# One joint gather of U and V rows, worked row by row, in the expert layer of a hybrid decoder trunk

## The reference

```
idx  = take_along_axis(cand_i, pos)            # token, head, 16 experts
gate = softmax(top_s)
act  = gelu(einsum('td,thkd->thk', xt, expert_u[idx]))
out  = einsum('thk,thkd->td', gate * act, expert_v[idx])
```

## Time and profile before

| | us |
|---|---|
| median of 3 runs | 4101.56 (4099.58 to 4101.72) |
| the profiled execution | 4101.73 |
| its span, first to last instruction | 4099.8 |

### The profile page before, as it was taken

One profiled execution on the slowest core, in us unless ns is written; L12 is line 12 of the kernel. 1 busy time (PEld: TensorE's weight loads), 2 busy tenths in 40 slices (PEclk: granted clock), 3 DMA queues, 4 the chain that ended last, 5 costly groups with the idle time before them and its releaser, 6 DMA issues. The chain is left out here.

```text
span 4099.8 us, 43527 instructions
## 1 busy us (share of the span) xinstructions
PE 3766.2 (92%) x15978; PEld 2821.7 (69%) x15978; DVE 2532.3 (62%) x5462; ACT 739.8 (18%) x1381; POOL 1789.6 (44%) x1508
## 2 busy tenths in 40 slices
PE   8999999987899999995799999999878999999947
PEld 7856788876666666652688567888766666666526
DVE  4455215838767676877844452158387677668777
...
GB/s 106 113 31 42 58 144 144 134 117 327 409 410 403 409 400 410 406 409 400 235 84 113 31 42 59 145 142 134 124 331 409 410 408 408 402 410 399 409 403 243
DMA packets 332164, 1047.19 MB, mean 255 GB/s; under 512 B 79024, under 2 KB 96048, under 8 KB 313008
## 3 DMA queue, kind: packets, MB, share of 16 engines
...
...
## 5 line engine op out<-in xcount | busy, mean ns | idle before, releaser
L1733 PE MATMUL bank<-v_tile,shared 128*128 128x512 f32 x2048 | 906.2, 597 | 31.9 <-DVE shared L2136 30.2
L2198 POOL DMA_INDIRECT u_rows<-in_peer_u,idx_all x512 | 673.6, 1316 | 541.1 <-DVE act_u L2093 444.5
L2105 DVE SCALAR_TENSOR_TENSOR x<-v_rows,act_w,x 128x1024 f32<-128x1024 f32 x512 | 657.8, 1285 | 349.9 <-DMA v_rows<-in_peer_v,idx_all 331.9
L2093 DVE CUSTOM_DVE_ANT_0 u_rows<-u_rows,h 128x1024 f32<-128x1024 f32 x512 | 610.0, 1221 | 194.8 <-DMA u_rows<-in_peer_u,idx_all 193.1
L1733 PEld LDWEIGHTS bank<-v_tile,shared 128*128 128x128 f32 x2048 | 391.6, 192 | 485.2 <-issue 444.6
L2198 POOL DMA_INDIRECT v_rows<-in_peer_v,idx_all x512 | 560.6, 1095 | 370.7 <-DVE x L2105 275.0
L2208 POOL DMA_INDIRECT first_cells<-first_gate,cell_all x256 | 412.6, 1612 | 593.4 <-DVEq L2085 467.0
L1721 PE MATMUL bank<-hT,bT 128*128 128x256 f32 x2048 | 452.5, 379 | 0.0
L1721 PEld LDWEIGHTS bank<-hT,bT 128*128 128x128 f32 x2048 | 388.4, 190 | 72.0 <-issue 22.0
L1625 PE MATMUL bank<-hT,ring 128*128 128x256 f32 x1536 | 341.6, 383 | 14.3 <-PEq L152 14.2
L1625 PEld LDWEIGHTS bank<-hT,ring 128*128 128x128 f32 x1536 | 293.9, 192 | 56.9 <-issue 16.2
(11 more groups left out here) (406 smaller groups left out, 4547.8 us busy)
## 6 DMA issues: line engine op xcount, KB each, us to landing
v_tile<-in_peer_v SPq DMA_DIRECT2D x256, 512.0 KB, 7.4
...
bT<-in_peer_ut SPq DMA_DIRECT2D x128, 512.0 KB, 8.1
...
```

Of the source, the lines that this page charges most:

```text
L1733: ins = mm(acc[t][part][:, :], act_pair[p % AHEAD][:, at:at + P], v_tile[:, e % DENSE, part * 512:part * 512 + 512], start=(e == 0), stop= ...
L2093: nc.vector.tensor_tensor_reduce(out=u[:, n % RINGS, :], in0=u[:, n % RINGS, :], in1=h[:, t, :], scale=1.0, scalar=0.0, op0=ALU.mult, op1= ...
L2105: stt(out=m.x[:, 2 + t, :], in0=vr[:, n % RINGS, :], scalar=act_w[:, p % 4, i:i + 1], in1=m.x[:, 2 + t, :], op0=ALU.mult, op1=ALU.add).the ...
L2198: nc.gpsimd.indirect_dma_start(out=rows[:, n % RINGS, :], out_offset=None, in_=table, in_offset=bass.IndirectOffsetOnAxis(ap=idx_all[:, t, ...
```

## The change

U and V are concatenated on the host to one table `peer_uv` with rows of 8 KB, and `u_rows` and `v_rows` become five joint buffers `uv_rows` of the same total size. One indirect DMA gathers both halves of a row (1 MB for 128 tokens). A buffer is freed by the add alone. DVE works rows one by one: dot n, then add n - 2 (ROWS_BEHIND = 2), where it did four dots and then four adds of two chunks before. ACT does, for each row, a gelu of one column and then the product with the gate as an activation Copy with a scale; DVE's product L2099 is gone. LAG falls to 1, which ends the list one chunk earlier. POOL's order follows: four joint gathers a chunk. The dense part is as before; it keeps its own tables of U and V.

```diff
--- before.py
+++ after.py
@@ -1394,7 +1394,9 @@
 HOT_CHUNKS = 4
 GATES_AFTER = 9
 CHUNKS_BESIDE = (0, 2, 4)
-LAG = 2
+LAG = 1
+ROWS = CHUNKS * STEP
+ROWS_BEHIND = 2
 CELLS = P * KEYS * P
 CELL_OCT = OCT * P
 LATE_CHUNKS = 4
@@ -1499,13 +1501,12 @@
 
     nc, io = m.nc, m.io
     with ExitStack() as ctx:
-        s = semaphores(m, COMMON + " wg_in keys_in gain_in p_in comb_ready rms_ready h_ready topped exp_done selected u_free v_free "
+        s = semaphores(m, COMMON + " wg_in keys_in gain_in p_in comb_ready rms_ready h_ready topped exp_done selected dotted weighed uv_free "
                        "first_chosen gelu_done out_free ple_rms ple_h ple_added slots_turned slots_here left_ready right_ready hot_filled hot_read "
                        "stored0 stored1 pre_in0 pre_in1 pre_in2 pre_in3 v_in0 v_in1 v_in2 v_in3 gate_in0 gate_in1 "
                        "pre_done pre_read gated v_done dense_added w_in side_sums last_sums last_scaled mix_filled mix_read")
         sb = lambda n, shape, dt=F32: ctx.enter_context(nc.sbuf_tensor(f"{n}_{layer}", shape, dt))
-        u = sb("u_rows", [P, RINGS, D])
-        vr = sb("v_rows", [P, RINGS, D])
+        uv = sb("uv_rows", [P, RINGS, 2 * D])
         h = sb("h", [P, 2, D])
         scores = sb("scores", [P, 4, 2, 2, KEYS])
         shared = sb("shared", [P, AHEAD, 2 * HALF_T])
@@ -1571,7 +1572,7 @@
         gate_in = s.gate_in0, s.gate_in1
         stored = s.stored0, s.stored1
         acc = (m.banks[4], m.banks[5]), (m.banks[6], m.banks[7])
-        tables = io.peer_u.rearrange("l e d -> (l e) d"), io.peer_v.rearrange("l e d -> (l e) d")
+        table = io.peer_uv.rearrange("l e d -> (l e) d")
         cols = lambda half: slice(half * HALF_T, (half + 1) * HALF_T)
         pre_bank = lambda p: m.banks[2 + p % 2 if p else 5]
         late_sum = lambda n: m.banks[4 + n // 2][:, cols(n % 2)]
@@ -1603,7 +1604,7 @@
         def arrivals(n):
 
             k = n % RINGS
-            return 16 * (layer * len(range(k, CHUNKS * STEP, RINGS)) + n // RINGS + 1)
+            return 16 * (layer * len(range(k, ROWS, RINGS)) + n // RINGS + 1)
 
         block = ctx.enter_context(nc.Block())
 
@@ -1904,9 +1905,16 @@
                         f(expo[:, t, :], top[:, t, :], ACT.Exp, bias=ntop[:, t:t + 1], accum_out=den[:, t:t + 1]).then_inc(s.exp_done, 1)
 
             def chunk(c):
-                if c < CHUNKS:
-                    act.wait_ge(s.u_free, STEP * (c + 1))
-                    f(act_g[:, c % 4, :], act_u[:, c % 4, :], ACT.Gelu_apprx_tanh).then_inc(s.gelu_done, 1)
+                if c == CHUNKS:
+                    return
+                for i in range(STEP):
+                    n = c * STEP + i
+                    t, col = slot(n)
+                    one = slice(i, i + 1)
+                    act.wait_ge(s.dotted, n + 1)
+                    f(act_g[:, c % 4, one], act_u[:, c % 4, one], ACT.Gelu_apprx_tanh).then_inc(s.gelu_done, 1)
+                    act.wait_ge(s.gelu_done, n + 1)
+                    f(act_w[:, c % 4, one], act_g[:, c % 4, one], ACT.Copy, scale=gate_all[:, t, col:col + 1]).then_inc(s.weighed, 1)
 
             def slots():
                 act.wait_ge(s.slots_turned, 1)
@@ -2084,29 +2092,31 @@
                     step.step(tt((gate_all if half else first_gate)[:, :, some], expo[:, :, :], over(rden.unsqueeze(2), (P, 2, TOPK)), ALU.mult))
                     v.sem_inc(s.selected if half else s.first_chosen, 1)
 
+            def dot(n):
+                t, _ = slot(n)
+                k = n // STEP % 4
+                v.wait_ge(m.uv_landed[n % RINGS], arrivals(n))
+                nc.vector.tensor_tensor_reduce(out=uv[:, n % RINGS, 0:D], in0=uv[:, n % RINGS, 0:D], in1=h[:, t, :], scale=1.0, scalar=0.0,
+                                               op0=ALU.mult, op1=ALU.add, accum_out=act_u[:, k, n % STEP:n % STEP + 1]).then_inc(s.dotted, 1)
+
+            def add_row(n):
+                t, _ = slot(n)
+                k = n // STEP % 4
+                v.wait_ge(s.weighed, n + 1)
+                if n:
+                    v.wait_ge(s.uv_free, n)
+                stt(out=m.x[:, 2 + t, :], in0=uv[:, n % RINGS, D:], scalar=act_w[:, k, n % STEP:n % STEP + 1], in1=m.x[:, 2 + t, :],
+                    op0=ALU.mult, op1=ALU.add).then_inc(s.uv_free, 1)
+                if n % TOPK == TOPK - 1:
+                    v.wait_ge(s.uv_free, n + 1)
+                    v.sem_inc(s.out_free, 1)
+
             def chunk(c):
-                if c < CHUNKS:
-                    for i in range(STEP):
-                        n = c * STEP + i
-                        t, col = slot(n)
-                        v.wait_ge(m.u_landed[n % RINGS], arrivals(n))
-                        nc.vector.tensor_tensor_reduce(out=u[:, n % RINGS, :], in0=u[:, n % RINGS, :], in1=h[:, t, :], scale=1.0, scalar=0.0,
-                                                       op0=ALU.mult, op1=ALU.add, accum_out=act_u[:, c % 4, i:i + 1]).then_inc(s.u_free, 1)
-                if LAG <= c < CHUNKS + LAG:
-                    p = c - LAG
-                    t, col = slot(p * STEP)
-                    v.wait_ge(s.gelu_done, p + 1)
-                    step.step(tt(act_w[:, p % 4, :], act_g[:, p % 4, :], gate_all[:, t, col:col + STEP], ALU.mult))
-                    for i in range(STEP):
-                        n = p * STEP + i
-                        v.wait_ge(m.v_landed[n % RINGS], arrivals(n))
-                        if n:
-                            v.wait_ge(s.v_free, n)
-                        stt(out=m.x[:, 2 + t, :], in0=vr[:, n % RINGS, :], scalar=act_w[:, p % 4, i:i + 1], in1=m.x[:, 2 + t, :],
-                            op0=ALU.mult, op1=ALU.add).then_inc(s.v_free, 1)
-                    if p % JOB_CHUNKS == JOB_CHUNKS - 1:
-                        v.wait_ge(s.v_free, STEP * (p + 1))
-                        v.sem_inc(s.out_free, 1)
+                for n in range(c * STEP, (c + 1) * STEP):
+                    if n < ROWS:
+                        dot(n)
+                    if ROWS_BEHIND <= n < ROWS + ROWS_BEHIND:
+                        add_row(n - ROWS_BEHIND)
 
             def hot(q):
                 if q == QUADS:
@@ -2187,18 +2197,16 @@
         @block.gpsimd
         def _(pool):
 
-            def fetch(n, free, rows, table, sems):
-                if not 0 <= n < CHUNKS * STEP:
-                    return
+            def fetch(n):
                 t, col = slot(n)
                 if n % TOPK == 0 and t == 0:
                     pool.wait_ge(s.selected, col // TOPK + 1)
                 if n >= RINGS:
-                    pool.wait_ge(free, n - RINGS + 1)
+                    pool.wait_ge(s.uv_free, n - RINGS + 1)
                 nc.gpsimd.indirect_dma_start(
-                    out=rows[:, n % RINGS, :], out_offset=None, in_=table,
+                    out=uv[:, n % RINGS, :], out_offset=None, in_=table,
                     in_offset=bass.IndirectOffsetOnAxis(ap=idx_all[:, t, col:col + 1], axis=0),
-                ).then_inc(sems[n % RINGS], 16)
+                ).then_inc(m.uv_landed[n % RINGS], 16)
 
             def scatter(n):
                 if n % TOPK == 0:
@@ -2214,14 +2222,11 @@
             for n in range(late):
                 scatter(n)
             for n in range(RINGS):
-                fetch(n, s.u_free, u, tables[0], m.u_landed)
-            for n in range(RINGS):
-                fetch(n, s.v_free, vr, tables[1], m.v_landed)
-            for c in range(CHUNKS + LAG):
-                for n in range(STEP * c + RINGS, STEP * (c + 1) + RINGS):
-                    fetch(n, s.u_free, u, tables[0], m.u_landed)
-                for n in range(max(STEP * (c - LAG), 0) + RINGS, STEP * (c - LAG + 1) + RINGS):
-                    fetch(n, s.v_free, vr, tables[1], m.v_landed)
+                fetch(n)
+            for c in range(CHUNKS):
+                begin = STEP * (c + 1) - ROWS_BEHIND - STEP + RINGS
+                for n in range(max(begin, RINGS), min(begin + STEP, ROWS)):
+                    fetch(n)
                 if c < LATE_CHUNKS:
                     for n in range(TOPK // LATE_CHUNKS):
                         scatter(late + c * TOPK // LATE_CHUNKS + n)
@@ -2237,9 +2242,9 @@
         m.nc, m.ctx, m.sems = nc, ctx, []
         names = "loaded stored x_landed0 x_landed1 x_landed2 x_landed3".split()
         m.once = once = namedtuple("Semaphores", names)(*[ctx.enter_context(nc.semaphore(n)) for n in names])
-        swdge = [ctx.enter_context(nc.semaphore(f"{n}_landed{k}")) for n in "uv" for k in range(RINGS)]
+        m.uv_landed = [ctx.enter_context(nc.semaphore(f"uv_landed{k}")) for k in range(RINGS)]
         m.scattered = ctx.enter_context(nc.semaphore("cells_scattered"))
-        m.nc, m.io, m.u_landed, m.v_landed = nc, io, swdge[:RINGS], swdge[RINGS:]
+        m.nc, m.io = nc, io
         m.banks = [ctx.enter_context(nc.psum_tensor(f"bank{k}", [P, 512], F32)) for k in range(8)]
```

(2 more changed lines are left out.)

## The result

The changed kernel takes 4205.1 us (median of four runs, 4197.7 to 4213.0) against 4101.6 us for the kernel before on the same chip: 1.0251 times as long, 95% interval 1.0229 to 1.0273, some 103 us. The sign and the range of the prediction hold, the size doesn't: 42 us were forecast.

What follows compares the result with a forecast made beforehand. PE was taken to set the pace up to about pair 59, then DMA, then DVE. Per layer +7 start, +8 cushion, +6 tail, -3.6 larger pieces, +3.6 slot waits: +21, twice +42 on 4101.7, 4144 us (range 4110 to 4190).

Steps and rivals of the forecast that it cites:

- five buffers are just enough in the dense stretch, with 7% to spare: Dense stretch: a chunk of gathered rows needs 16.7 us with five joint buffers, under PE's 17.9, so PE hides it.
- latency rival: Dense stretch: gathers take 10 to 14 us to land and bound the kernel; about 4260 us, at 12 some 4500; chance 0.18.
- Larger pieces, -3.6: Last nine DMA-bound chunks: 8 KB pieces move 4% faster, saving 3.6 us a layer; elsewhere PE hides the gain.
- Start, +7: Before PE's dense work: six more adds (7.7 us) precede the last one-hot products; +7 us a layer, from -5 to +20.
- the coupling: ACT's in-order list: a chunk's small gelu stands behind a dense gelu that waits for PE's value products.
- Cushion, +8: Last dense pairs: DVE's lead over PE is capped at 45 us instead of 56.6, costing 8 us a layer (4 to 12).
- Slot waits, +3.6: Chunks where DMA was kept full before now wait a little for a free joint buffer: +3.6 us a layer.
- L: Time from a 1 MB gather's issue to its landing: 6 us in the tail, 8 beside dense traffic.
- the prediction's own formula: Joint buffers: three row times must cover landing time plus 2.85 us; a chunk takes four row times plus 2.3 us.
- Tail, +6: Six chunks after the dense work: 84 us against 78, from buffer waits and a 4.4 us stall; +6 a layer (0 to +15).
- faster rival: Whole kernel: DMA is the real bound and the lead's cap never binds; -16 us a layer, 4070 us; chance 0.18.
- The rule weighed: Gate table's store: queues alternate by packet, so 8 KB pieces could stretch 26 us to 46; kept as an upper end.

## Why the prediction was right in sign and wrong in size

**The step that failed** is the overlap that was to hide the joint buffers: "five buffers are just enough in the dense stretch, with 7% to spare". The sum put the slots at +3.6 us a layer, set off by -3.6 for larger pieces, and the start and the cushion at 7 and 8 for the new order. The kernel with separate buffers splits the measured +48 otherwise (second layer, us):

| step | start | 0 to 51 | 51 to 63 | to last add | together |
|---|---|---|---|---|---|
| shorter lag alone | +6 | 0 | +16 | -18 | +4 |
| rows one by one, with ScalarE | +7 | 0 | +2 | 0 | +9 |
| joint buffers, filled by one gather | +6 | +4 | +13 | +11 | +35 |

In the first layer the three sums are +1, +10 and +37. So lag and order, which were to cost most, come to 12 and 13 us a layer, and the joint buffers, which were to cost nothing beside PE and DMA and a part of the tail's 6, to 35 and 37. The terms that gave the sign are thus the small ones. The range held because it took in the lower part of the latency rival, not because the forecast's own terms came near.

**POOL.** Right: its work halved and nothing came of it.

**Larger pieces, -3.6.** The direction was right. Where the engines are full, 8 KB rows run at 418 instead of 409 GB/s, 2% where I took 4. In the changed kernel itself they are never full behind the 52nd pair (0.97), so the gain isn't cashed.

**Start, +7.** Measured +19 and +21. The term had one of three parts: the adds ahead of the one-hot products, which the kernel with the shorter lag puts at +6. The row order adds 7 (155.5 against 148.1, separate buffers): its last store of the gate table is issued 87.6 us behind the first dot, 80.1 with the lag alone. What delays it wasn't taken apart; the forecast had allowed 4 us for the small gelus ahead of it. The joint buffers add 6 more (161.2; with one more gather under way 157.6). I looked for what delays the store and its load, and took it that "PE then runs without a gap": after the change the chain is no longer store and load. The waits of 12.25 and 11.17 us for ACT were not in my list, though I had named the coupling; I followed it only from PE to DVE. The store is issued 15 us later than before relative to the first dot, where 10 were forecast, and took 26.2 us.

**Cushion, +8.** Measured +21 and +31 between the pairs 51 and 63. Of that the shorter lag alone makes +7 and +16, given back in the tail; the row order adds 2, the joint buffers 13. I took the cap of the lead, 45 us, for the lead itself. The cap held from the tenth pair on (43 us at most), but at the 40th, 48th and 52nd pair the lead was 25 to 31. ACT also waits for other work of PE than the dense gelus, as the query copy at 3272.02 (20.0 us), which fits this. And I charged only the cushion. Without ScalarE in the rows those pairs take 107.5 us, so beside joint buffers the lock is worth 22 us; with the add one row behind 114.5, so the slots are worth 15; without both 96.7, so 33 together. The slots were to cost nothing there, hidden by DMA.

**Slot waits, +3.6.** L beside dense traffic was taken as 8 us. The view of L2206 (POOL's gathers) from 3250 us to the end says

```profile
DMA to landing us min/median/max: 5.4/8.8/12.3
```

In the long stretch alone, from 3280 to 3780 us, the median is 9.2, and from 4083 to 4169 us 6.9:

```profile
uv_rows<-in_peer_uv,idx_all POOLq DMA_INDIRECT x113, 9.2
```

```profile
uv_rows<-in_peer_uv,idx_all POOLq DMA_INDIRECT x21, 6.9
```

So L was 15% too small in both places. With 9.2 the prediction's own formula gives T = 4.02 and 4 x 4.02 + 2.3 = 18.4 us a chunk, more than PE's 17.9, where it had 16.7; the chunks 8 to 47 take 18.5. It is not a proof of the formula: without ScalarE in the rows the same five buffers give 18.0. For chunks 48 to 57 the median of 8.8 makes T = 3.88, where they show 3.87; but before the change they took 3.93 us a row, with the DMA engines full, so nothing is lost in them. What the chunks 8 to 47 lose, 21 us, costs TensorE 4 us at once; the rest shows behind the 52nd pair, where the lead is missing.

**Tail, +6.** The predicted stall, behind ACT's wait for PE and its table load, is there, 4.07 us where 4.4 was forecast:

```profile
4122.33 1.28 DVE L2108 SCALAR_TENSOR_TENSOR x<-uv_rows,act_w,x 128x1024 f32<-128x1024 f32 x1 [4.07 <-ACT act_w L1917]
...
4124.67 1.28 DVE L2108 SCALAR_TENSOR_TENSOR x<-uv_rows,act_w,x 128x1024 f32<-128x1024 f32 x1
4125.87 1.22 DVE L2099 CUSTOM_DVE_ANT_0 uv_rows<-uv_rows,h 128x1024 f32<-128x1024 f32 x1
```

Yet the tail came out at -6 and +2, because I had forgotten what the shorter lag gives back there: 12 and 18 us (106.1 and 106.5 with the lag alone, against 117.7 and 124.4). Against that the tail grows by 14 and 11 us, 11 of them with the joint buffers, where 6 were forecast. (With T = 2.95 a chunk is 11.8 us, not 11.4.) I also missed that the new order saves DVE time: four adds in a row take 1.39 us each, as the prediction has them, while an add between two dots takes 1.20, as at 4124.67 us.

**The rivals.** The latency rival, at 0.18, had the right mechanism, at L = 10 and a price of 68 us a layer. At 9.2 the joint buffers cost 35 to 37 a layer; the kernel with the add one row behind gives 38 of the 103 us back. The 456 us of one buffer less show how near that edge the kernel stands. The faster rival, at 0.18, named stalls under 1 us on ACT as its condition; they were up to 20.4 us. That the rows are cut to 4 KB packets is excluded by the packet count.

**The rule weighed.** The store took 26.2 us, not 46. The last store of a layer took 21.6 and 21.8 us with four buffers (two gathers under way), 26.2 and 28.2 with five and 28.9 and 29.0 with four and the add one row behind (three in both), and 30.9 and 31.7 with five and the add one row behind (four). The Trainium skill (DMA: Bandwidth & Descriptors, Queues, rings and completion order) has the engines take turns between queues, packet by packet. With that rule the runs agree in direction: more gathers queued beside it, a longer store; my reason for taking the low end held. The agreement that the prediction found with 26.4 us is that of one store, though: in the kernel before the four stores of the second layer take 20.6, 13.3, 18.8 and 26.4 us.
